# The latents' two columns computed inside the decay mixer's levels, with residual tiles kept in device memory meanwhile

## The reference

```
h = rms_norm(x) ; cols = h @ w_in          # one wide product, split into columns
y_gdn  = gated delta rule, both directions, chunks of 64   (6 heads)
y_mla  = attention over latents:  q = norm(cq) @ w_uq ; k, v = norm(ckv) @ w_ukv   (6 heads)
y_rwkv = recurrence with a learned decay, both directions  (4 heads)
mix = concat(y_gdn, y_mla, y_rwkv) * silu(gate column)
x = x + mix @ w_out
```

## Time and profile before

| what | value |
|---|---|
| median of three runs | 1974.73 us (1974.01 to 1977.77) |
| profiled execution | 1975.6 us |
| its span | 1973.8 us |
| mean granted clock of PE | 0.954 of full speed |
| PE busy (products) | 1702.0 us, 86% of the span |
| DVE, ACT, POOL busy | 857.7, 647.6, 269.5 us |
| layer 0 and layer 1 of the second block | about 835 to 1400 us and 1400 to 1955 us |
| chain that ended last | PE 73%, DVE 12% |

### The profile page before, as it was taken

How to read it: one execution, slowest core, us unless ns; L and a number is a source line. 1 busy time by engine, 2 the same in 40 slices (tenths; PEclk the granted TensorE clock), 3 DMA queues, 4 the chain that set the end, 5 groups by cost and what they waited for, 6 DMA issues and landing times.

```text
span 1973.8 us, 44313 instructions
## 1 busy us (share of the span) xinstructions
PE 1702.0 (86%) x17970; PEld 952.2 (48%) x17970; DVE 857.7 (43%) x1514; ACT 647.6 (33%) x1158; POOL 269.5 (14%) x330
## 2 busy tenths in 40 slices
PE   5998895987787777897988789999998897799996
PEld 2444543544443444444665664354445655653452
DVE  1567524111111111276866763151357848642331
ACT  3314611000000000135544635252246536433442
POOL 0002211111111111004331200000002303000001
PEclk8998996999999999999999899999999998999998
DMA  9759015999999999701000003110211000012101
GB/s 358 268 192 303 1 43 213 365 422 423 426 424 425 423 424 423 305 33 49 31 3 2 3 5 126 43 43 33 81 43 35 4 2 2 4 66 105 43 1 43
DMA packets 75100, 307.77 MB, mean 156 GB/s; under 512 B 10908, under 2 KB 22300, under 8 KB 57888
## 3 DMA queue, kind: packets, MB, share of 16 engines
q1 hardware_dynamic: 63280, 291.98, 37.6%
q0 software_dynamic: 5360, 9.33, 1.3%
q10 hardware_dynamic: 6272, 3.81, 0.6%
HBM read 301.01 MB, written 16.52 MB: 161 GB/s over the span
## 4 chain that ended last, share of the span: by engine, by line
PE 73%; DVE 12%; another core or an unknown queue 6%; ACT 4%; issue 3%; ACTq 1%; DMA 1%; DVEq 0%; POOL 0%; POOLq 0%
PE bank L509 13%; PE bank L2368 12%; PE bank L2384 6%; PE bank L1079 6%; PE bank L568 4%; PE bank L2206 3%; PE bank L2290 3%; PE bank L1050 2%; PE bank L561 2%; PE bank L525 2%; ACT arena L1091 1%; PE bank L2230 1%; PE bank L2218 1%; PE bank L549 1%
## 5 line engine op out<-in xcount | busy, mean ns | idle before, releaser
L509 PE MATMUL bank<-hT,arena 128*128 128x512 f32 (+1 forms) x640 | 286.9, 604 | 3.8 <-ACTq L1092 2.4
L2368 PE MATMUL bank<-arena 128*64 128x256 f32 x1792 | 214.9, 397 | 68.2 <-remote 68.2
L2368 PEld LDWEIGHTS bank<-arena 128*64 128x64 f32 x1792 | 134.4, 142 | 159.0 <-issue 108.5
L509 PEld LDWEIGHTS bank<-hT,arena 128*128 128x128 f32 (+1 forms) x640 | 122.5, 193 | 161.1 <-issue 156.5
L2974 DVE COPY arena<-bank 128x256 f32<-128x256 f32 x32 | 13.6, 424 | 329.4 <-PE bank L2376 329.4
L568 PE MATMUL bank<-hT,arena 128*128 128x512 f32 x224 | 121.7, 657 | 8.5 <-ACTq L1092 6.8
L2384 PE MATMUL bank<-arena 128*64 128x512 f32 x448 | 104.0, 606 | 16.4 <-remote 16.4
L2628 ACT ACTIVATE arena<-bank 128x512 f32<-128x512 f32 x32 | 19.1, 597 | 294.8 <-PE bank L2384 294.8
L1091 ACT ACTIVATE arena<-bank 128x512 f32<-128x512 f32 (+2 forms) x124 | 73.2, 590 | 117.7 <-PE bank L509 79.4
L1079 PE MATMUL bank<-arena 128*128 128x512 f32 x256 | 110.4, 593 | 0.0
L549 PE MATMUL bank<-arena 64*64 64x64 f32 x3200 | 73.1, 233 | 24.8 <-DVE arena L1841 10.3
(11 more groups left out here) (459 smaller groups left out, 2966.6 us busy)
## 6 DMA issues: line engine op xcount, KB each, us to landing
arena<-w_gate SPq DMA_DIRECT2D x28, 2048.0 KB, 30.4
arena<-w_up SPq DMA_DIRECT2D x28, 2048.0 KB, 21.0
arena<-w_down SPq DMA_DIRECT2D x28, 2048.0 KB, 26.3
arena<-w_ada SPq DMA_DIRECT2D x12, 2048.0 KB, 20.0
arena<-w_in SPq DMA_DIRECT2D x10, 2048.0 KB, 9.4
arena<-w_out SPq DMA_DIRECT2D x6, 2048.0 KB, 7.8
arena<-w_in SPq DMA_DIRECT2D x6, 1536.0 KB, 6.5
hT<-w_up SPq DMA_DIRECT2D x4, 2048.0 KB, 20.9
```

The lines of the kernel that those rows point to most:

```text
L509: m = pe.matmul(bank[b][0:w, :], slot2(n)[:, k, c:c + w], hT[:, k, :], start=(k == 0), stop=(k == KD - 1))
L2368: mm = pe.matmul(bank[b][c * CAP:(c + 1) * CAP, 0:FE // 2], XT[j][:, k % 4, k // 4, :], e_slot(e_at(e, i), KD)[:, k, c * (FE // 2):(c + 1) ...
```

## The change

The two latent columns are computed in the decay mixer's levels instead of the tail, one matmul at a time. Their weights cannot lie in a slot then, so six of the eight tiles of the residual are written to device memory (`x_d`, 1.5 MB) once they are settled; four of the freed tiles take the weights (`latent_w`), two take the raw columns (`latent_raw`). After ACT has copied the latents out, the six tiles are read back, and DVE waits for them before it adds the output. Bank 6 holds the column that is being summed: it is free between the chunk products of a pair and the next use. Gates 0 to 3 are moved up one place each and use banks 0, 1, 5 and 3.

```diff
@@ SP
                 for n in range(1, 5):
                     unit(n)
+                take(sp, sem("x_settled"))
+                sp.dma_start(x_d, xT[:, 0:AWAY, :]).then_inc(sem("x_spilled"), 16)
+                take(sp, sem("x_spilled"), 16)
+                c, w = UNITS2[5]
+                src = w_in2[bass.ds(l, 1), :, c:c + w].rearrange("a (k p) n -> p (a k) n", p=P)
+                sp.dma_start(latent_w, src).then_inc(sem("latent_w_full"), 16)
                 take(sp, sem("ring_free"))
-                unit(5)
                 unit(6)
+                unit(7)
                 take(sp, sem("go_sp"))
...
+                take(sp, sem("latents_moved"))
+                sp.dma_start(xT[:, 0:AWAY, :], x_d).then_inc(sem("x_back"), 16)
-                for n in range(7, 10):
+                for n in range(8, 10):
                     unit(n)
@@ PE, rwkv_chunks (here l is the level)
+                def latent_within(ct, k):
+                    if k == 0:
+                        pe.wait_ge(sem("r_k_free"), 2 + 2 * ct)
+                        take(pe, bank_free[6])
+                        if ct == 0:
+                            take(pe, sem("latent_w_full"), 16)
+                    m = pe.matmul(bank[6][:, :], latent_w[:, k, ts(ct)], hT[:, k, :], start=(k == 0), stop=(k == KD - 1))
+                    if k == KD - 1:
+                        m.then_inc(for_act[6], 1)
                 for ct in range(2):
+                    if ct == 1:
+                        pe.wait_ge(bank_free[6], 1)
...
                             crossed(d, r_Bn[d], r_bt[:, ct, d]).then_inc(sem(f"g_v_done{d}"), 1)
+                            if d == 0 and l > 1:
+                                latent_within(ct, 2 * l - 3)
...
                             crossed_back(d, Y, V, l == LEVELS - 1).then_inc(sem(f"g_t_done{d}"), 1)
+                            if d == 0 and l < LEVELS - 1:
+                                latent_within(ct, 2 * l - 2)
@@ PE, tail
                 mean(0)
-                take(pe, slot_full[1], 16)
-                latents(0, 0, 128)
+                gate(0, 0)
                 mean(1)
...
-                latents(1, 128, 128)
                 norm_over_heads(1)
                 o_free.clear()
-                gate(0, 5)
-                gate(1, 3)
+                gate(1, 1)
+                gate(2, 5)
...
-                gate(2, 6)
+                gate(3, 3)
...
                 for i in range(3):
                     queries(i, 3 + i, for_dve)
-                gate(3, 7)
@@ ACT, end of each head pair's levels
+                    move(6, latent_raw[:, ct, :], bank[6][:, :])
@@ ACT, tail
-                move(0, m_cq[:, 0, :], bank[0][:, :])
-                take(act, for_act[1])
-                chain(act.activation(m_cq[0:64, 1, :], bank[1][0:64, :], ACT.Copy))
-                chain(act.activation(m_ckv[0:64, 0, :], bank[1][64:128, :], ACT.Copy))
-                act.sem_inc(bank_free[1], 1)
-                act.sem_inc(slot_free[1], 1)
+                chain(act.activation(m_cq[:, 0, :], latent_raw[:, 0, :], ACT.Copy))
+                chain(act.activation(m_cq[0:64, 1, :], latent_raw[0:64, 1, :], ACT.Copy))
+                chain(act.activation(m_ckv[0:64, 0, :], latent_raw[64:128, 1, :], ACT.Copy))
+                act.sem_inc(sem("latents_moved"), 1)
...
-                gate(0, 5)
-                gate(1, 3)
-                gate(2, 6)
+                gate(0, 0)
+                gate(1, 1)
+                gate(2, 5)
...
-                gate(3, 7)
+                gate(3, 3)
@@ DVE, before the output is added
+                take(dve, sem("x_back"), 16)
```

More of the change, by code:

```diff
@@ L76 @@
 N_IN2 = 3448
+AWAY = 6
 C_DECAY = float(np.exp(-0.5))
@@ L163, in build @@
                       "pool_w_loaded", "scores_done", "pooled", "params_loaded", "choices_full", "h_stored", "h_ready",
-                      "x_loaded", "y_stored", "routed", "y_summed", "mod_ready", "rs_ready", "scaled", "pad_zero")
+                      "x_loaded", "y_stored", "routed", "y_summed", "mod_ready", "rs_ready", "scaled", "pad_zero", "gain_moved", "probs_free0",
+                      "probs_free1", "last_full", "x_full0")
         for late, early in zip(("g_rk_full0", "g_rk_full1", "g_uw_free0", "g_uw_free1", "r_in_full", "r_bt_full", "r_k_free",
@@ L167, in build @@
                                 "r_sa_full", "ring_free", "kk_full", "g_w_done", "x_tiles", "g_e_in0", "g_e_in1", "g_pt_full0",
-                                "g_pt_full1"), first_only):
+                                "g_pt_full1", "x_settled", "x_spilled", "latent_w_full", "latents_moved", "x_back"), first_only):
             sems[late] = sem(early)
@@ L174, in build @@
         y_d = nc.dram_tensor("y_scratch", (2 * T, D), F32).ap()
+        x_d = nc.dram_tensor("x_scratch", (AWAY * P, T), F32).ap().rearrange("(k p) t -> p k t", p=P)
         xT = sb("xT", [P, KD, T])
@@ L343, in build @@
         rs_final = mix[:, 0, :]
+        latent_w = xT[:, 0:4, :].rearrange("p a b -> p (a b)").rearrange("p (k n) -> p k n", k=KD)
+        latent_raw = xT[:, 4:AWAY, :]
         def const2(name, rows=P):
@@ L982, in pe_second @@
                 o_free = Count(pe, sem("g_o_free"))
-                def latents(i, c, w):
-                    take(pe, bank_free[i])
-                    column(i, 5, c, w).then_inc(for_act[i], 1)
                 def gate(i, b):
@@ L1168, in act_second @@
             for l in range(LAYERS):
+                more_layers = l < LAYERS - 1
                 inverse_lengths()
@@ L1459, in act_second @@
                 chain.reset()
+                if more_layers:
+                    act.sem_inc(sem("x_settled"), 1)
             inverse_lengths()
@@ L1483, in pool_second @@
                 chain(pool.tensor_tensor(xT[:, k, :], xT[:, k, :], rs_final, ALU.mult))
+            pool.sem_inc(sem("x_settled"), 1)
             chain.reset()
```

## The result

| | before | after |
|---|---|---|
| median of the runs | 1975.64 us (1974.01 to 1977.77, 4 runs) | 1950.05 us (1948.58 to 1952.48, 4 runs) |
| profiled execution, its span | 1975.6, 1973.8 us | 1952.48, 1950.6 us |
| mean granted clock | 0.954 | 0.966 |

The ratio is 0.9884 [0.9865, 0.9902] (the interval holds the true ratio in 95 of 100 cases), which is some 23 us less; the two medians of the table are 25.6 us apart. The forecast was 1950.5 us, in a range from 1943 to 1963.

A forecast was written before the change was run, and what follows sets the result against it. PE was taken as full in the tail: -31.3 us there, +2 x 3.3 for the second pair's levels, 0 for the first, +2 x 0.3 for late weights, -24.1 in all; forecast 1950.5 us, range 1943 to 1963.

The forecast's parts named there:

- The tail: Decay mixer to attention: two latent columns, the bank 6 wait and slow gate time go, 31.3 us less over both layers.
- the gap before gate 2: Tail: PE's wait for ACT to read bank 6 goes, 0.95 us in layer 0 and 1.0 in layer 1.
- The hands: Tail: operands ready before PE wants them, sums of squares with 1.6 us in hand, scaled latents with 1.2.
- The second pair's levels: Decay mixer, second head pair: fills lengthen a level from 3.47 to 4.30 us in four intervals, 3.3 us a layer.
- The first pair: Decay mixer, first head pair: fills hidden under VectorE, taken as 0, bounds -2.3 to 7.0 us a layer.
- The rival of the kept clock: First head pair's levels: fills hold the higher clock, -2.3 us a layer, 1946 us in all; chance 15%.
- The first gate's weights: Before the first gate: unit 6 lands 0 to 2.2 us late a layer, taken as 0.3.
- The other reading: Gate weights after the recurrence: one queue's descriptors start in order, unit 6 lands as if alone, lateness 0 instead of 0.3.
- The transfers: Spill, latent weights and restore: covered and given no price; weights in SBUF near 955, wanted around 1107.

The follow-up runs named there:

- e5: The changed kernel with gate 3 in bank 6 instead of bank 3: 1955.96 us, ratio 0.9910.
- e3: The kernel before the change, each latent column in the tail cut to one product of eight, nothing moved: 1964.01 us, ratio 0.9956.
- e6: The changed kernel with the length product over the second decay output put behind gate 1 instead of before it: 1973.63 us, ratio 0.9998.
- e2: The changed kernel with only the last of eight latent products computed in the second head pair's levels: 1951.77 us, ratio 0.9880.
- e1: The changed kernel with only the last of eight latent products computed in the first head pair's levels: 1951.02 us, ratio 0.9887.
- e4: The kernel before the change plus spill, latent weights' load and restore, latents still computed in the tail: 1981.39 us, ratio 1.0044.
- e12: The changed kernel itself measured once more: 1951.13 us, ratio 0.9893 to the kernel before.
- e8: The changed kernel with spill and latent weights started only after the delta mixer's recurrence in both layers: 1951.39 us, ratio 0.9887.
- e10: The changed kernel with spill and latent weights after the delta recurrence in layer 0, right behind unit 1 in layer 1: 1947.87 us, ratio 0.9879.
- e9: The changed kernel with both fills of a level behind crossed_back and none behind crossed: 1963.82 us, ratio 0.9955.
- e7: The changed kernel with weight unit 7 issued before unit 6 after the decay recurrence: 1969.2 us, ratio 0.9983.

## Why the prediction was right, step by step

**The tail** was forecast at -31.3 us and is -31.4 in the traces: -16.6 and -14.7 by its terms, -16.4 and -15.0 measured. Two columns out of a full engine, the wait for bank 6 and its gate at the lower clock account for it; e5 puts the wait back and gets 1.3 and 2.9 us. Two readings were a little off: the x16 of a column is 16 matmul records and not 8 loads and 8 products, which leaves the 0.859 us a product as it is; and the gap before gate 2 was 1.21 us by PE's timeline in both layers, not 0.95 and 1.0, since the chain's row of 4.20 us takes in 0.26 us of it (the sums and the turned tile now take 2.97 + 0.97). The gate behind them takes 7.06 and not 6.87. That 13.7 us could go in full rests on the moved gates and the earlier norm, and this is shown from both sides: e3 removes the length and keeps the places (40 to 50% of the worth), e6 keeps all and delays one product (a third of the tail's gain is left, and nothing of the net gain).

**The hands** of 1.6 and 1.2 us were 1.8 and 1.1. ACT's logarithm moved from 1209.91 to 1205.15 in a kernel whose tail starts 1.65 us later: 6.4 us earlier relative to the first gate's place, 6.5 forecast.

**The second pair's levels**: 4.30 us forecast from the delta mixer, 4.29 and 4.30 measured. The pair as a whole grew from 17.60 to 20.43, 2.8 us, and by e2 2.1 to 2.3 for seven fills, against 3.3: the four intervals cost what they should, and what follows the last level starts a little sooner relative to it.

**The first pair** was forecast at 0 and took 0.5 us less in layer 0 (53.7 against 54.2, to the second pair's first crossed product) and 1.1 in layer 1 (54.3 against 55.3), which is within its scatter. The rival of the kept clock was half right: the clock stands at 1.00, and e1 shows that the fills hold it there, but as DVE has the pace the -2.3 us did not come.

**The first gate's weights** were forecast 0.3 us late in each layer and were in time. The other reading, that the first transfer lands nearly as if alone, was the right one.

**The transfers** are the step that failed: "in SBUF near 955, wanted only in the decay mixer's levels" is true, and the sum took it for free. The spill and the weights cost +3.3 and +3.6 us in the delta mixer of the profiled execution, and e4 shows 8.7 us for all the transfers by themselves. The levels came out 2.4 us cheaper than forecast (in part the scatter of layer 1), the weights 0.6, and the first block happened to be 4.1 shorter in that execution. That the sum -24.1 met -23.2 in the traces is therefore in part luck. Without the first block the traced change is -19.1; the ratio gives -23 (e12: -21), with an interval of some 3.7 us to each side. So the forecast of the total is right within what the runs can tell, with one term missing that is as large as the whole forecast price of the levels.

**What the pauses are.** The page lists a queue of kind "instruction" (q8); near the pauses it moves one packet of 16 KB about every 4 us, in which PE has some 250 matmuls and weight loads. The view of the transfers (queue: packets, MB, share) for three windows: the kernel before from 943.40 to 945.00; then the kernel after from 935.69 to 942.50, where q8 has no row, and from 942.50 to 943.70.

```profile
q8 instruction: 1, 0.02, 5.6%
```

```profile
q1 hardware_dynamic: 1336, 2.40, 96.1%
```

```profile
q8 instruction: 1, 0.02, 5.3%
```

Put beside the next fill of PE (the first after the two above), this packet starts 0.1 us before to 0.1 us after it in the four traces that have neither the spill nor the latents' weights there (before, e3, e8, e10), and 2.3 to 3.5 us after it in the ten that have. It then starts 0.5 to 2.4 us before the spill has landed. And the ends of the pauses follow the packets: in the kernel after the two packets end at 943.62 and 948.79, and the pauses at 944.98 and 950.17. In all fourteen traces PE has 80 pauses of over 0.33 us in the second block that no semaphore accounts for, and every one ends 1.15 to 1.55 us after the end of such a packet, though the packets lie some 4 us apart. So PE had run out of instructions; beside the spill and the weights their packets came late.

**What stays open.** The pauses lie in passes of small products, in the same places in two kernels (behind the 22nd and the 17th recorded entry of a pass), and the long ones in layer 0 come with spill and weights and go with them (e8, e10). That the packets are late there is shown; by what rule the engines serve the two queues is not, and no run put the bulk transfer in smaller pieces to see whether the packets then come in time. Of the +3.3 us, 2.2 are located in the stretch shown; where the rest lies is not. Nor is it known why layer 1's is 0 in one execution and 3.6 in another.

## What to carry to other kernels

Work taken out of a stretch in which one engine is full is worth its full length only if something else covers what that engine will reach sooner: list every operand that comes next, with the time at which it is ready and the time at which it will be wanted, before counting the gain. Work put into another stretch costs by what sets the pace there: next to nothing beside a full DVE, 0.83 us a level where PE closed the loop. The place within the level counts too (e9): in another place the same fills cost 6 us more a layer, a little by a DVE operation left uncovered, the most with a lower clock. A transfer that nobody waits for is not free beside dense small products, because PE's instructions come as transfers too; it should be measured alone, as in e4, before it is counted at nothing.

## What the runs showed of the hardware beyond that

A wait of PE costs more than its length: 4.3 us became 10.5 (e6), 5.3 became 8.1 (e7), two waits of 2.6 ate 6.4 to 7.1 of 12.0 (e3). Part of what follows the wait runs at the lower clock, so that the gate that takes 6.87 us took 9.33 (granted clock 0.76) and 9.71 (0.73). Even the wait of 1.21 us before gate 2 in the kernel before was followed by a gate of 8.82 us in layer 0 (granted clock 0.81), while the same wait in layer 1 was followed by one of 7.13 (1.00). Transfers of 1.5 and 1 MB beside passes of 64x64 products made pauses of 0.4 to 2.5 us in PE, which no semaphore explains and which end 1.15 to 1.55 us after an instruction packet. And the same program's first block took from 829.6 to 835.7 us from one execution to the next, which is why a single span cannot settle a question of 4 us.
